# Gate/up pairs with five quads of seven products instead of four, in a two-layer encoder trunk

## The chip, the core and the metric

The kernel runs on one core of a Trainium2 chip. The metric is the device time of one execution in microseconds (us). The engines of the core that matter here are TensorE (PE, matrix products; PEld its weight loads), VectorE (DVE), ScalarE (ACT), GpSimd (POOL) and SyncE (SP), which issues most of the DMAs. Each has its own stream of instructions in program order, and they wait for each other through semaphores.

## The reference

The reference is a trunk of two layers on 256 tokens of width 2048, in float32. Each layer normalizes, projects, does differential attention in eight heads and a short gated convolution, projects back, and then does a SwiGLU block with an inner width of 5632. The change touches that block alone:

```python
h = rmsnorm(x, norm_ffn[l])
x = x + (jax.nn.silu(h @ w_gate[l]) * (h @ w_up[l])) @ w_down[l]
```

All products are float32. The kernel gets this accuracy from three products of a reduced kind (float32r): with each operand split into a high part (rounded) and a low part (the rest), it adds high x high, high x low and low x high.

## The kernel before

**Blocks, units and parts.** A weight matrix is cut into blocks of 512 columns, and a block into units of 256 rows (two tiles of 128). In the gate/up matrix a block holds 256 gate and 256 up columns, and two blocks, left and right, make a pair; there are 11 pairs in each layer and eight units in a block. For a unit SyncE loads a tile of 128 x 1024 into `raw`, ScalarE rounds it into `whi` (the high part, `split`, L761), VectorE subtracts and writes `wlo` (the low part, `split`, L1184), and TensorE does its products with both (L1861 to L1863): 3 for each of two tiles and two halves of the tokens, 12 for a unit and 24 for the same unit of left and right. There are four places in `raw` (each of four tiles, 1 MB) and five slots in `whi` and `wlo`, taken in turn.

**Quads.** Some units of left and right are taken together as a quad, which needs seven block products instead of eight (21 matmuls instead of 24, L1873 to L1875), as in Strassen's scheme. For this the sums of weight tiles must be made and split too. One quad has four steps on VectorE: `first_parts` (low parts of 1024 and of 512), `first_sum` (L1199, 512, into `raw`), `other_sums` (L1206, 1024, into `raw`) and `second_parts` (two low parts of 1024 of what the sums left there). The low parts of a quad stand at L1191 and the matching high parts, by ScalarE, at L767. The sum of two right tiles is made by a DMA that adds into `raw`, issued by GpSimd (`add_b`, L687) once the tile h has landed. The matching sums of the normed tokens are called forms. They are made once in a layer, in batches of two quads, by `form_sums` and `form_low` (VectorE) and `form_high` (ScalarE), in the last two blocks of the output projection, and lie where later pairs write their results.

**Order of a pair.** Of the 11 pairs the first nine after the first (1 to 9) are alike: four quads (units 0 to 3) and the units 4 to 7 of both sides; pair 0 differs in its head, pair 10 has two quads. The orders are written out by hand, once for each engine (`gu_four` and `gu_rest`), and must agree in the order in which slots are taken. VectorE begins a pair with the end of the one before it: `gu_fold` (L1281 to L1285), which puts the seven sums together as soon as ScalarE has copied the first of them out of PSUM (`sum_out`, L818), `gates_ups` (L1295) and `hidden_products` (L1558). GpSimd makes two low parts in a pair, unit 4 of left and of right (L693, `split_first_units`), once that same sum has been copied, and in between the adding DMAs. After `gu_rest` the next pair follows; then the down projection, which has its own quads.

Of the kernel before, what the change touches and what calls it, by code (L numbers as in the profile page):

```python
# [30 lines left out]
NCH = DM // COLS  # L31
# [24 lines left out]
GU_SEVENS = 4  # L56
DOWN_SEVENS = 10
FORM_BATCH = 2
GU_BATCHES = -(-GU_SEVENS // FORM_BATCH)
GU_FIRST_ORDER = [("left", 4), ("right", 4), ("left", 5), ("first", 0), ("first", 1), ("second", 0), ("first", 2),  # L60
# [5 lines left out]
GU_FOURS = range(1, NGU // 2 - 1)  # L66
POOL_UNIT = 4
# [109 lines left out]
class Pair:  # L177
    def __init__(self, plan, i, blocks, order, turns=None):
# [6 lines left out]
        self.first, self.fours = order is GU_FIRST_ORDER, order in (GU_FIRST_ORDER, GU_FOUR_ORDER)  # L185
        self.quad_loads = {}
        if self.fours:
            self.load_four(plan)
        for part, k in order:
            if part == "first":  # L190
                q = self.quads[k] = Quad(self, k)
                q.number = plan.quads
                plan.quads += 1
                q.loads = self.quad_loads[k] if self.fours else plan.next_place()
                plan.places[q.raw()] += 1
                q.added = plan.places[q.raw()]
# [3 lines left out]
            else:  # L200
                plan.unit(blocks[part == "right"], k, by_pool=self.fours and not self.first and k == POOL_UNIT)

        self.sums_taken = plan.taken[max(q.split[-1] for q in self.quads.values())][1]

    def load_four(self, plan):

        def place_of_units(k, place):
            for half, block in enumerate(self.blocks):
                block.load[k] = Load(plan, place, half)

        def place_of_quad(k, place):
            self.quad_loads[k] = [Load(plan, place, 0), Load(plan, place, 1)]
# [5 lines left out]
        place_of_units(4, a)  # L218
        place_of_quad(0, b)
        place_of_quad(1, c)  # L220
        place_of_units(5, d)
        place_of_quad(2, a)
        self.blocks[0].load[6] = Load(plan, d, 0, whole=False)
        place_of_quad(3, b)
        self.blocks[1].load[6] = Load(plan, d, 1, whole=False)
        place_of_units(7, c)
        plan.rotation = [a, d, b, c]


class Plan:  # L230
    def __init__(self):
# [15 lines left out]
        for layer in range(DEPTH):  # L247
            for name, n, by_tokens, units in (("qk", NQK, False, UNITS), ("v", NV, True, UNITS),
# [3 lines left out]
                for i in range(n):  # L252
# [7 lines left out]
                    elif i % 2:  # L260
                        if name == "gu":
                            pair = Pair(self, i // 2, made[-2:], GU_FOUR_ORDER if i // 2 in GU_FOURS
                                        else GU_LAST_ORDER if i == NGU - 1 else GU_FIRST_ORDER)
# [39 lines left out]
def build_program(nc, x, x_t_d, w_in, w_out, w_gu, w_down, consts_d, lambdas_d, tables_d, ident_d, gain_d, out):  # L303
# [49 lines left out]
    def share(name, shape, dtype):  # L353
# [44 lines left out]
               "gu": [(shared_end - 4 * FORM, shared_end - 2 * FORM, 2), (shared_end - 8 * FORM, shared_end - 6 * FORM, 2)]}  # L398
# [143 lines left out]
    with nc.Block() as block:  # L542

        @block.sync
        def _(sp):
# [69 lines left out]

            first, second = plan.blocks[:2]
# [14 lines left out]
            for blk in plan.blocks[2:]:  # L631
                if isinstance(blk, Pair) and blk.fours:
                    load_four(blk)
                elif isinstance(blk, Pair):
# [11 lines left out]
        def _(pool):  # L646
# [49 lines left out]
            def split_first_units(prior, pair):  # L696
                pool.wait_ge(sum_copied, prior.number + 1)
                for blk in pair.blocks:
                    split(blk, POOL_UNIT)

            pool.wait_ge(set_up, 2)
            for layer in range(DEPTH):
# [46 lines left out]
        def _(act):  # L749
# [159 lines left out]
            def gu_rest(pair):  # L909
# [12 lines left out]
                split(right, 7, 8)  # L922
                sum_out(pair)

            def gu_four(pair, prior):
# [4 lines left out]
                split(left, 4, 5)  # L930
                split(right, 4, 5)
# [11 lines left out]
                split(left, 5, 6)  # L943
                gu_rest(pair)
# [53 lines left out]
            for layer in range(DEPTH):  # L998
# [92 lines left out]
                for c in range(1, NCH):  # L1091
# [6 lines left out]
                    if c >= NCH - GU_BATCHES:  # L1098
                        split(blk, 6, 7)
                        form_high(layer, "gu", c - (NCH - GU_BATCHES))  # L1100
# [18 lines left out]
                for p in GU_FOURS:  # L1119
                    prior, pair = pair, plan.pairs[layer, "gu", p]  # L1120
                    gu_four(pair, prior)
# [57 lines left out]
        def _(dve):  # L1179
# [142 lines left out]
            def gu_rest(pair):  # L1322
# [18 lines left out]
                split(left, 7, 8)  # L1341
                split(right, 7, 8)
                gu_fold(pair)
                gates_ups(pair, 0, 0)

            def gu_four(pair, prior):
# [17 lines left out]
                split(left, 5, 6)  # L1364
                hidden_low(layer, before[1])
                gu_rest(pair)
# [232 lines left out]
            for layer in range(DEPTH):  # L1599
# [111 lines left out]
                for c in range(1, NCH):  # L1711
# [5 lines left out]
                    if c >= NCH - GU_BATCHES:  # L1717
                        split(blk, 4, 6)
                        form_sums(layer, "gu", c - (NCH - GU_BATCHES))
# [562 lines left out]
```

## Time and profile before

| what | value |
|---|---|
| device time, median of 3 runs | 2156.34 us |
| lowest, highest | 2155.99 us, 2157.56 us |
| span of the profiled execution | 2155.3 us |
| TensorE busy | 2144.2 us, 99% |
| VectorE busy | 1771.7 us, 82% |
| ScalarE busy | 1218.7 us, 57% |
| GpSimd busy | 314.5 us, 15% |
| a middle gate/up pair, fold to fold | 41.74 us |

The profile is of one execution, whose own time is the span, 1.0 us under the median of the timed runs. Busy time is the time covered by an engine's instructions. Two instructions that follow each other in an engine's pipeline overlap in their records, so the pace of an engine is read from the distance of their starts. The idle time in front of an instruction is given in brackets, with the instruction that released it.

### The profile page before, as it was taken

The numbers are of one execution on the slowest core, as the hardware profiler recorded it, in microseconds if no ns is written. First come the engines' busy times: TensorE is split into PE (matmuls) and PEld (weight loads), VectorE is DVE, ScalarE is ACT, GpSimd is POOL, SyncE is SP. The second block draws the span as 40 slices with busy tenths as digits, with TensorE's granted clock in tenths as the row PEclk, the third lists the DMA queues.
The fourth block names the chain that finished last, engine by engine and source line by source line (L and its number), as shares of the span: only waits on it lengthen the run. The fifth ranks groups of instructions, "written<-read, shape, count | busy, mean of one in ns | idle before, by whom it ended". The sixth has DMA issues, their size and how long they took to land.

```text
span 2155.3 us, 27924 instructions
## 1 busy us (share of the span) xinstructions
PE 2144.2 (99%) x10397; PEld 1794.4 (83%) x10397; DVE 1771.7 (82%) x2143; ACT 1218.7 (57%) x1714; POOL 314.5 (15%) x310
## 2 busy tenths in 40 slices
PE   9999999999999999999999999999999999999998
PEld 7888888888888888888888888888888888888886
DVE  5776676899899988999866666768998998988997
ACT  6454455666566555556554555546665665655564
POOL 0031120211221110000001211201112112100010
PEclk9999999999999999999999999999999999999999
DMA  9654445777777776767766444557777777756685
GB/s 349 203 183 176 176 157 189 212 218 223 246 217 229 227 229 205 227 216 221 246 200 217 171 161 157 176 194 212 218 229 232 219 222 244 221 198 219 219 240 181
DMA packets 152872, 456.81 MB, mean 212 GB/s; under 512 B 17440, under 2 KB 18080, under 8 KB 152352
## 3 DMA queue, kind: packets, MB, share of 16 engines
q1 hardware_dynamic: 132624, 416.41, 55.5%
q0 software_dynamic: 18816, 35.66, 9.8%
q10 hardware_dynamic: 1296, 2.94, 0.4%
q8 instruction: 83, 1.36, 0.2%
q14 instruction: 53, 0.43, 0.1%
HBM read 448.65 MB, written 2.10 MB: 209 GB/s over the span
## 4 chain that ended last, share of the span: by engine, by line
PE 97%; DVE 1%; ACT 1%; DMA 1%; POOL 0%; issue 0%; ACTq 0%; SPq 0%; DVEq 0%
PE bank L1861 16%; PE bank L1863 16%; PE bank L1862 16%; PE bank L1835 14%; PE bank L1875 9%; PE bank L1874 9%; PE bank L1873 9%; PE bank L1838 7%; PE bank L2039 1%; PE bank L1998 1%; PE bank L2021 1%; PE bank L1977 0%; DMA raw<-w_gu_dram 0%; POOL o_rms L675 0%; DVE wlo L1191 0%; PE bank L2007 0%
## 5 line engine op out<-in xcount | busy, mean ns | idle before, releaser
L761 ACT ACTIVATE whi<-raw 128x1024 fp32r<-128x1024 f32 x540 | 553.9, 1056 | 195.2 <-PE bank L1863 137.4
L1184 DVE TENSOR_TENSOR wlo<-raw,whi 128x1024 fp32r<-128x1024 f32 x504 | 606.9, 1229 | 65.9 <-ACT whi L761 64.9
L767 ACT ACTIVATE whi<-raw 128x1024 fp32r<-128x1024 f32 x480 | 430.0, 944 | 241.7 <-DVE raw L1206 139.6
L1191 DVE TENSOR_TENSOR wlo<-raw,whi 128x1024 fp32r<-128x1024 f32 x480 | 501.0, 1084 | 49.7 <-ACT whi L767 46.4
L1835 PE MATMUL bank<-xg,whi 128*128 128x512 f32 x1280 | 406.9, 399 | 1.0 <-DVE wlo L1440 1.0
L1861 PE MATMUL bank<-whi,xg 128*128 128x512 f32 x864 | 339.3, 393 | 0.5 <-DVE wlo L1184 0.5
L1863 PE MATMUL bank<-whi,xg 128*128 128x512 f32 x864 | 336.7, 390 | 0.0
L1862 PE MATMUL bank<-wlo,xg 128*128 128x512 f32 x864 | 336.5, 389 | 0.0
L1838 PEld LDWEIGHTS bank<-xg,wlo 128*128 128x128 f32 x1280 | 240.5, 188 | 56.9
L1838 PE MATMUL bank<-xg,wlo 128*128 128x256 f32 x1280 | 252.0, 278 | 0.0
L1835 PEld LDWEIGHTS bank<-xg,whi 128*128 128x128 f32 x1280 | 195.0, 189 | 3.3 <-DVE xg L1434 1.4
L1861 PEld LDWEIGHTS bank<-whi,xg 128*128 128x128 f32 x864 | 162.3, 188 | 34.8 <-DVE wlo L1184 1.6
L1863 PEld LDWEIGHTS bank<-whi,xg 128*128 128x128 f32 x864 | 162.2, 188 | 33.9
L1862 PEld LDWEIGHTS bank<-wlo,xg 128*128 128x128 f32 x864 | 162.3, 188 | 32.6
L687 POOL DMA_DIRECT2D raw<-w_gu_dram x84 | 72.6, 864 | 747.6 <-DMA raw<-w_gu_dram 747.6
L1861 PE MATMUL bank<-whi,hidden 128*128 128x512 f32 x416 | 162.5, 391 | 0.0
L1863 PE MATMUL bank<-whi,hidden 128*128 128x512 f32 x416 | 161.9, 389 | 0.0
L1862 PE MATMUL bank<-wlo,hidden 128*128 128x512 f32 x416 | 161.9, 389 | 0.0
L1206 DVE TENSOR_TENSOR raw<-raw 128x1024 f32<-128x1024 f32 x120 | 145.9, 1215 | 0.9
L1873 PE MATMUL bank<-whi,form_hi_gu 128*128 128x512 f32 x336 | 130.7, 389 | 0.0
L1875 PE MATMUL bank<-whi,form_lo_gu 128*128 128x512 f32 x336 | 130.7, 389 | 0.0
L1874 PE MATMUL bank<-wlo,form_hi_gu 128*128 128x512 f32 x336 | 130.7, 389 | 0.0
(161 smaller groups left out, 3050.7 us busy)
## 6 DMA issues: line engine op xcount, KB each, us to landing
raw<-w_gu_dram SPq DMA_DIRECT2D x268, 512.0 KB, 4.9
raw<-w_in_dram SPq DMA_DIRECT2D x188, 512.0 KB, 4.5
raw<-w_down_dram SPq DMA_DIRECT2D x140, 512.0 KB, 5.4
raw<-w_gu_dram SPq DMA_DIRECT2D x168, 256.0 KB, 4.2
raw<-w_out_dram SPq DMA_DIRECT2D x64, 512.0 KB, 4.4
raw<-w_gu_dram POOLq DMA_DIRECT2D x84, 256.0 KB, 5.7
raw<-w_down_dram SPq DMA_DIRECT2D x72, 256.0 KB, 4.7
raw<-w_down_dram POOLq DMA_DIRECT2D x36, 256.0 KB, 6.1
```

Of the source, the lines that this page charges most:

```text
L761: act.activation(whi[:, blk.slot(k)], raw[:, slot, half * UNIT_KT:(half + 1) * UNIT_KT, :], ACT.Copy).then_inc(hi_ready, 1)
L767: act.activation(whi[:, quad.slot(n), 0:tiles.stop - tiles.start], raw[:, quad.raw(), tiles, :], ACT.Copy).then_inc(hi_ready, 1)
L1184: dve.tensor_tensor(wlo[:, blk.slot(k)], raw[:, slot, half * UNIT_KT:(half + 1) * UNIT_KT, :], lo_bits(whi[:, blk.slot(k)]), ALU.subtract) ...
L1191: dve.tensor_tensor(wlo[:, quad.slot(n), into], raw[:, quad.raw(), tiles, :], lo_bits(whi[:, quad.slot(n), into]), ALU.subtract).then_inc( ...
L1835: pe.matmul(b[j][:], whi[:, blk.slot(k), i, w[j]], moving[:, kt, :], start=(kt == 0), stop=False, skip_group_check=True)
L1838: done = pe.matmul(b[j][:, 0:S], wlo[:, blk.slot(k), i, w[j]], moving[:, kt, 0:S], start=False, stop=final, skip_group_check=True)
L1861: pe.matmul(b[:], x_hi, w_hi, start=(n == UNIT_KT * blk.first_unit), stop=False)
L1862: pe.matmul(b[:], x_hi, w_lo, start=False, stop=False)
L1863: done = pe.matmul(b[:], x_lo, w_hi, start=False, stop=final)
L1873: pe.matmul(into[:], x_hi, w_hi, start=start, stop=False)
L1874: pe.matmul(into[:], x_hi, w_lo, start=False, stop=False)
L1875: return pe.matmul(into[:], x_lo, w_hi, start=False, stop=stop)
```

## The change

Pairs 1 to 8 of each layer take five quads instead of four (units 0 to 4) and units 5 to 7 instead of 4 to 7, in a new order on all engines (`GU_FIVE_ORDER`, `gu_five_rest`) and with a new order of the places in `raw` (`load_five`). Pair 9 keeps four quads. A third batch of forms, for the fifth quad alone, is made at the end of pair 0. GpSimd makes unit 5 of both sides as it made unit 4, and also the low part of right 7 of a pair with five quads: `split_last_unit` waits until VectorE has made that of left 7.

```diff
-GU_SEVENS = 4
+GU_SEVENS = 5
...
+GU_FIVE_ORDER = [("left", 5), ("right", 5), ("first", 0), ("first", 1), ("left", 6), ("second", 0), ("first", 2),
+                 ("second", 1), ("first", 3), ("right", 6), ("second", 2), ("first", 4), ("second", 3), ("second", 4),
+                 ("left", 7), ("right", 7)]
+GU_MIDDLE = range(1, NGU // 2 - 1)
+GU_FIVES = range(1, NGU // 2 - 2)
...
+    def load_five(self, plan):
+
+        a, b, c, d = plan.rotation
+        self.place_of_units(plan, 5, a)
+        self.place_of_quad(plan, 0, b)
+        self.place_of_quad(plan, 1, c)
+        self.place_of_quad(plan, 2, d)
+        self.place_of_units(plan, 6, a)
+        self.place_of_quad(plan, 3, b)
+        self.place_of_quad(plan, 4, c)
+        self.place_of_units(plan, 7, d)
...
+            def split_last_unit(pair):
+                left, right = pair.blocks
+                wait_for_split(pool, left.split[UNITS - 1])
+                split(right, UNITS - 1)
...
-                for p in GU_FOURS:
+                for p in GU_MIDDLE:
                     prior, pair = (plan.pairs[layer, "gu", n] for n in (p - 1, p))
                     add_b(pair.quads[0])
+                    if prior.fives:
+                        split_last_unit(prior)
                     split_first_units(prior, pair)
...
                 second_parts(q3)
                 split(left, 7, 8)
+                if pair.first:
+                    form_sums(pair.layer, "gu", GU_BATCHES - 1)
                 split(right, 7, 8)
+                if pair.first:
+                    form_low(pair.layer, "gu", GU_BATCHES - 1)
                 gu_fold(pair)
...
+            def gu_five_rest(pair):
+
+                left, right = pair.blocks
+                q0, q1, q2, q3, q4 = (pair.quads[k] for k in range(5))
+                first_sum(q1)
+                second_parts(q0)
+                first_parts(q2)
+                other_sums(q1)
+                second_parts(q1)
+                first_sum(q2)
+                first_parts(q3)
+                other_sums(q2)
+                split(right, 6, 7)
+                second_parts(q2)
+                first_sum(q3)
+                first_parts(q4)
+                other_sums(q3)
+                second_parts(q3)
+                first_sum(q4)
+                other_sums(q4)
+                second_parts(q4)
+                split(left, 7, 8)
+                gu_fold(pair)
+                gates_ups(pair, 0, 0)
```

VectorE in the middle of such a pair before the change, around the sums of q1 (L1206 is other_sums, L1184 the low part of a unit, L1191 those of a quad, L1199 first_sum):

```order
L1191 TENSOR_TENSOR wlo<-raw,whi 128x512 [waits hi_ready]
L1206 TENSOR_TENSOR raw<-raw 128x2x512 [waits first_sums,weights_ready]
L1184 TENSOR_TENSOR wlo<-raw,whi 128x1024 [waits hi_ready]
L1191 TENSOR_TENSOR wlo<-raw,whi 128x1024 [waits hi_ready] x2
L1199 TENSOR_TENSOR raw<-raw 128x512 [waits b_added0,weights_ready]
```

The same place of a pair with five quads in the changed program (L1272 is other_sums, L1257 a quad's low parts, L1265 first_sum):

```order
L1257 TENSOR_TENSOR wlo<-raw,whi 128x512 [waits hi_ready]
L1272 TENSOR_TENSOR raw<-raw 128x2x512 [waits first_sums,weights_ready]
L1257 TENSOR_TENSOR wlo<-raw,whi 128x1024 [waits hi_ready] x2
L1265 TENSOR_TENSOR raw<-raw 128x512 [waits b_added3,weights_ready]
L1257 TENSOR_TENSOR wlo<-raw,whi 128x1024 [waits hi_ready]
```

The low part of right 5 is gone from between the sums of q1 and its second parts; what follows them is as before.

VectorE at the end of a pair before the change, from q2's second parts to the fold (L1281):

```order
L1191 TENSOR_TENSOR wlo<-raw,whi 128x1024 [waits hi_ready] x2
L1199 TENSOR_TENSOR raw<-raw 128x512 [waits b_added3,weights_ready]
L1184 TENSOR_TENSOR wlo<-raw,whi 128x1024 [waits hi_ready]
L1206 TENSOR_TENSOR raw<-raw 128x2x512 [waits first_sums,weights_ready]
L1191 TENSOR_TENSOR wlo<-raw,whi 128x1024 [waits hi_ready] x2
L1184 TENSOR_TENSOR wlo<-raw,whi 128x1024 [waits hi_ready] x2
L1281 TENSOR_TENSOR gate_up<-gate_up,bank 128x512 [waits sum_copied]
```

The same stretch with five quads, from the last of q4's first parts to the fold (L1250 is the low part of a unit, L1347 the fold):

```order
L1257 TENSOR_TENSOR wlo<-raw,whi 128x512 [waits hi_ready]
L1272 TENSOR_TENSOR raw<-raw 128x2x512 [waits first_sums,weights_ready]
L1257 TENSOR_TENSOR wlo<-raw,whi 128x1024 [waits hi_ready] x2
L1265 TENSOR_TENSOR raw<-raw 128x512 [waits b_added2,weights_ready]
L1272 TENSOR_TENSOR raw<-raw 128x2x512 [waits first_sums,weights_ready]
L1257 TENSOR_TENSOR wlo<-raw,whi 128x1024 [waits hi_ready] x2
L1250 TENSOR_TENSOR wlo<-raw,whi 128x1024 [waits hi_ready]
L1347 TENSOR_TENSOR gate_up<-gate_up,bank 128x512 [waits sum_copied]
```

A second set of sums, that of q4, with its second parts has come in behind q3's, and one low part of a unit instead of two stands in front of the fold.

GpSimd in a middle pair before, with the two low parts at its head (L693) and the adding DMAs (L687):

```order
L693 TENSOR_TENSOR wlo<-raw,whi 128x1024 [waits hi_ready,sum_copied]
L693 TENSOR_TENSOR wlo<-raw,whi 128x1024 [waits hi_ready]
L687 DMA raw<-w_gu_dram 128x512 [waits h_landed3]
L687 DMA raw<-w_gu_dram 128x512 [waits h_landed0]
L687 DMA raw<-w_gu_dram 128x512 [waits h_landed2]
L687 DMA raw<-w_gu_dram 128x512 [waits h_landed1]
```

GpSimd in the changed program, from the last adding DMA of a pair with five quads (L724) through the DMA of the next pair's q0 and the three low parts (L730):

```order
L724 DMA raw<-w_gu_dram 128x512 [waits h_landed1]
L730 TENSOR_TENSOR wlo<-raw,whi 128x1024 [waits hi_ready,weights_ready]
L730 TENSOR_TENSOR wlo<-raw,whi 128x1024 [waits hi_ready,sum_copied]
L730 TENSOR_TENSOR wlo<-raw,whi 128x1024 [waits hi_ready]
L724 DMA raw<-w_gu_dram 128x512 [waits h_landed2]
L724 DMA raw<-w_gu_dram 128x512 [waits h_landed3]
L724 DMA raw<-w_gu_dram 128x512 [waits h_landed1]
```

The low part of right 7 stands behind the DMA of the next pair's first quad and ahead of the two that were there; it waits for VectorE (weights_ready), and only the next one for the copied sum.

## Rows read from the trace of the kernel before

**Rows 1.** The page: busy time by engine, and the chain of waits by engine.

```profile
PE 2144.2 (99%) x10397; PEld 1794.4 (83%) x10397; DVE 1771.7 (82%) x2143; ACT 1218.7 (57%) x1714; POOL 314.5 (15%) x310
...
PE 97%; DVE 1%; ACT 1%; DMA 1%; POOL 0%; issue 0%; ACTq 0%; SPq 0%; DVEq 0%
```

**Rows 2.** Windows of two middle pairs, fold to fold: busy us by engine.

```profile
589.88:631.62 41.74, 41.74 (x190) 34.58 (x189) 38.23 (x43) 25.36 (x32) 8.17 (x6) 1.00 0.74 227
631.62:673.37 41.75, 41.75 (x190) 34.59 (x189) 38.24 (x44) 25.36 (x32) 8.20 (x6) 1.00 0.74 228
```

**Rows 3.** Timeline of TensorE: start and length in us, line, operation.

```profile
628.07 0.39 PE L1873 MATMUL bank<-whi,form_hi_gu 128*128 128x512 f32 x1
...
630.57 0.39 PE L1875 MATMUL bank<-whi,form_lo_gu 128*128 128x512 f32 x1
```

**Rows 4.** Timeline of VectorE, the end of a middle pair, idle in brackets.

```profile
620.94 0.68 DVE L1199 TENSOR_TENSOR raw<-raw 128x512 f32<-128x512 f32 x1
621.54 1.22 DVE L1184 TENSOR_TENSOR wlo<-raw,whi 128x1024 fp32r<-128x1024 f32 x1
622.68 1.22 DVE L1206 TENSOR_TENSOR raw<-raw 128x1024 f32<-128x1024 f32 x1
625.07 2.36 DVE L1191 TENSOR_TENSOR wlo<-raw,whi 128x1024 fp32r<-128x1024 f32 x2 [1.17 <-ACT whi L767]
627.35 2.35 DVE L1184 TENSOR_TENSOR wlo<-raw,whi 128x1024 fp32r<-128x1024 f32 x2
631.62 0.69 DVE L1281 TENSOR_TENSOR gate_up<-gate_up,bank 128x512 f32<-128x512 f32 x1 [1.92 <-ACT gate_up L818]
```

**Rows 5.** Timeline of VectorE, the same pair from its fold on.

```profile
589.88 0.69 DVE L1281 TENSOR_TENSOR gate_up<-gate_up,bank 128x512 f32<-128x512 f32 x1 [1.90 <-ACT gate_up L818]
...
605.26 4.08 DVE L1191 TENSOR_TENSOR wlo<-raw,whi 128x1024 fp32r<-128x1024 f32 x4
609.26 1.21 DVE L1206 TENSOR_TENSOR raw<-raw 128x1024 f32<-128x1024 f32 x1
...
616.27 1.22 DVE L1206 TENSOR_TENSOR raw<-raw 128x1024 f32<-128x1024 f32 x1
...
618.66 2.36 DVE L1191 TENSOR_TENSOR wlo<-raw,whi 128x1024 fp32r<-128x1024 f32 x2
```

**Rows 6.** Timeline of ScalarE in the same pair.

```profile
610.55 3.48 ACT L767 ACTIVATE whi<-raw 128x1024 fp32r<-128x1024 f32 x4 [1.56 <-PE bank L1875]
...
623.98 2.01 ACT L767 ACTIVATE whi<-raw 128x1024 fp32r<-128x1024 f32 x2 [3.42 <-DVE raw L1206]
```

**Rows 7.** Timeline of GpSimd, its two low parts of that pair.

```profile
590.94 4.77 POOL L693 TENSOR_TENSOR wlo<-raw,whi 128x1024 fp32r<-128x1024 f32 x2 [4.11 <-ACT whi L761]
```

**Rows 8.** Hidden products by line in that pair: ns min, median, max.

```profile
L1558 DVE SCALAR_TENSOR_TENSOR ev<-gate_up,rms_tok,ev x4: 468/471/701, 595.3 to 597.8; 128x256 f32<-128x256 f32 x4
```

**Rows 9.** A quad's h load by its line, L583, in the pairs.

```profile
DMA to landing us min/median/max: 2.6/3.0/5.2
```

**Rows 10.** A quad's left load by its line, L585, in the pairs.

```profile
DMA to landing us min/median/max: 3.7/5.4/6.7
```

**Rows 11.** Timeline of VectorE in the first gate/up pair.

```profile
391.75 0.68 DVE L1199 TENSOR_TENSOR raw<-raw 128x512 f32<-128x512 f32 x1
392.54 1.23 DVE L1206 TENSOR_TENSOR raw<-raw 128x1024 f32<-128x1024 f32 x1
...
422.89 0.69 DVE L1281 TENSOR_TENSOR gate_up<-gate_up,bank 128x512 f32<-128x512 f32 x1 [1.75 <-ACT gate_up L818]
```

**Rows 12.** Groups by form, two steps of the gate/up forms: busy, mean.

```profile
L1274 DVE TENSOR_TENSOR form_lo_gu<-form_sum_gu,form_hi_gu 128x1024 fp32r<-128x1024 f32 x4 | 4.9, 1226 | 0.0
...
L1258 DVE TENSOR_TENSOR ev<-xg 128x1024 f32<-128x1024 f32 x4 | 4.9, 1219 | 0.0
```

**Rows 13.** Windows of the last stretches: PEclk is the granted clock.

```profile
2145.00:2150.00 5.00, 2.12 (x10) 1.43 (x8) 2.99 (x7) 1.76 (x3) 1.88 (x2) 1.00 0.26 105
2150.00:2155.00 5.00, 0.00 (x0) 0.00 (x0) 0.75 (x1) 1.15 (x1) 0.00 (x1) 0.67 0.79 315
```

More of the change, by code:

```diff
@@ L200, in __init__, with place_of_units, place_of_quad @@
             else:
-                plan.unit(blocks[part == "right"], k, by_pool=self.fours and not self.first and k == POOL_UNIT)
+                plan.unit(blocks[part == "right"], k, by_pool=(part, k) in self.pool_units)
         self.sums_taken = plan.taken[max(q.split[-1] for q in self.quads.values())][1]
-    def load_four(self, plan):
[L207 to L212, printed above, removed]
+    def place_of_units(self, plan, k, place):
+        for half, block in enumerate(self.blocks):
+            block.load[k] = Load(plan, place, half)
+    def place_of_quad(self, plan, k, place):
+        self.quad_loads[k] = [Load(plan, place, 0), Load(plan, place, 1)]
+    def load_four(self, plan):
         if self.first:
@@ L614, in load_four, with load_five @@
                 load(right, 7)
+            def load_five(pair):
+                left, right = pair.blocks
+                load(left, 5)
+                load(right, 5)
+                for k in range(3):
+                    load_quad(pair.quads[k])
+                load(left, 6)
+                load(right, 6)
+                load_quad(pair.quads[3])
+                load_quad(pair.quads[4])
+                load(left, 7)
+                load(right, 7)
             first, second = plan.blocks[:2]
@@ L929, in gu_four @@
                 before = [b.i for b in prior.blocks]
-                split(left, 4, 5)
-                split(right, 4, 5)
+                k = 5 if pair.fives else 4
+                split(left, k, k + 1)
+                split(right, k, k + 1)
                 silu(prior.layer, before[0], 0)
@@ L2056, in gu_rest, with gu_five_rest, gu_middle @@
                 plain(right, 7)
-            def gu_four(pair):
+            def gu_five_rest(pair):
                 left, right = pair.blocks
-                plain(left, 4)
+                q0, q1, q2, q3, q4 = (pair.quads[k] for k in range(5))
+                second_products(q0)
+                first_products(q2)
+                second_products(q1)
+                first_products(q3)
+                plain(right, 6)
+                second_products(q2)
+                first_products(q4)
+                second_products(q3)
+                second_products(q4)
+                plain(left, 7)
+                plain(right, 7)
+            def gu_middle(pair):
+                left, right = pair.blocks
+                k = 5 if pair.fives else 4
+                plain(left, k)
                 turn_hidden(pair.layer, 2 * pair.i - 2)
-                plain(right, 4)
+                plain(right, k)
                 turn_hidden(pair.layer, 2 * pair.i - 1)
```

105 lines of the change are left out of this document (70 added, 35 removed).

## The prediction

> **What bounds the kernel now.** I read the page first: TensorE is busy 99% of the span and the chain of waits is 97% TensorE [rows 1]. Then the windows of two middle gate/up pairs, from one fold on VectorE to the next: 41.74 and 41.75 us, with TensorE busy in all of it and VectorE in 38.23 and 38.24 [rows 2]. The reader is to see two things there. A pair lasts as long as its matmuls; and VectorE, which makes nearly all low parts, has only some 3.5 us to spare.
>
> That TensorE sets the pair is better seen in the timeline than in its busy share, because its records overlap: the first and the last of twelve matmuls start 2.50 us apart, so they follow each other every 0.227 us though each is recorded with 0.39 [rows 3]. A middle pair has four quads of 21 products and four unit pairs of 24, 180 in all: 40.9 us, and the eight transposes of the hidden blocks fill the rest of 41.74.
>
> Next the timeline of VectorE at the end of such a pair [rows 4]. A low part of 1024 starts 1.14 us after the one before (621.54 to 622.68), two take 2.28 (625.07 to 627.35), a 512 one 0.60 (620.94 to 621.54). VectorE stands still in two places that matter: 1.92 before the fold, which waits for ScalarE's copy of a sum that TensorE finishes late, and 1.17 at 625.07, which is the row to remember. There other_sums(q3) (L1206) is followed directly by second_parts(q3) (L1191). The second parts are split from what other_sums has just written, and ScalarE must round them first: it starts at 623.98, 0.08 after other_sums ends [rows 6], and VectorE goes on 1.09 later. From other_sums to the next low part are 2.39 us (622.68 to 625.07) in which VectorE works 1.22. For q0, q1 and q2 another low part stands in between and covers this: for q2 the same 2.39 (616.27 to 618.66) hold other_sums and a whole unit [rows 5].
>
> **The change, part by part.**
>
> TensorE. In each of the 16 pairs (8 in each layer) one unit pair of 24 products becomes a quad of 21: 3 x 0.227 = 0.68 us off, a pair of 41.06, 10.9 us in all. This is a gain only where TensorE stays the bound.
>
> VectorE, work. The pair loses three 1024 low parts (right 5 of old, left or right 6, and right 7, that goes to GpSimd; units left to it fall from six to three): 3 x 1.14 = 3.42. It gains a quad: three 1024 low parts, one of 512, first_sum of 512 and other_sums of 1024: 4 x 1.14 + 2 x 0.60 = 5.76. Net 2.34 us more, on 38.23: 40.6 of the 41.06 that TensorE would need. Taken alone that would just fit.
>
> VectorE, stalls. The new order has only one unit left between the sums, right 6, and it covers q2. Behind other_sums of q1, q3 and q4 the second parts follow directly, so the 1.17 comes three times instead of once: 2.34 us more. This is in the order of the code, and ScalarE cannot start sooner than the sums are written. Together 4.7 us more in a pair with 3.5 us of idle time, and the 1.17 in these cannot be used up. So VectorE, with ScalarE's copies in its loop, is the new bound, and I follow it from fold to fold on the clock of the pair in [rows 4, 5].
>
> Fold at 589.88; up to 605.26 the order is as before with left 6 in the place of left 5: 15.38 us. Second parts of q0 and first parts of q2 up to 609.26, 4.00, also as before. From there:
> - q1: other_sums and stall 2.39, second parts 2.28: 613.93.
> - first_sum(q2) 0.60 and first parts of q3, 4.00 - 2.28 = 1.72: 616.25.
> - other_sums(q2) and right 6, 2.39; second parts of q2, 2.28: 620.92.
> - first_sum(q3) and first parts of q4, 2.32: 623.24.
> - q3: 2.39 + 2.28: 627.91.
> - first_sum(q4), at once followed by other_sums(q4), which reads it: 0.79 as in the first pair (391.75 to 392.54) [rows 11]: 628.70. other_sums and stall 2.39, second parts 2.36 to the end of the second: 633.45.
> - TensorE gets the first of these two at 632.31, starts 0.08 later and works twelve products; the twelfth starts 11 x 0.227 after, at 634.89. In the trace the fold starts 1.05 after such a twelfth (630.57 to 631.62) [rows 3, 4]. VectorE's low part of left 7 lies beside this.
> The fold comes at 635.94 instead of 631.62: 4.32 us later in each pair, 16 x 4.32 = 69.1 us. TensorE is then idle some 5 us in each pair, mainly before q3 and q4 and in front of right 6.
>
> The third batch of forms stands in the first pair of each layer between VectorE's last two low parts, where the fold then waits 1.75 us [rows 11]. For two quads the batch has steps of 1.22 and 1.23 [rows 12], one of 512 elements at 0.69 and two smaller ones, at most 4.5 together; for one quad it is between half and all of that, 2.2 to 4.5. I take 2.7, near the half, since the part of a step that doesn't shrink is small in the rows (1.22 against 0.68 for half the elements). Less the 1.75, it puts that fold off by 0.95; twice, 1.9 us (bounds 0.9 to 5.5).
>
> GpSimd. It makes two low parts in 4.77 [rows 7] and gets a third, right 7. It may start when left 7 is through, 634.5, and not when the sum is copied, so its three end near 634.6 + 7.16 = 641.8, 5.8 us behind the fold, as the two do now (595.71, behind 589.88). TensorE wants right 7 twelve products after left 7, at 637.8, and gets it at 637.0. Cost 0, with 0.8 us of cover. Ahead of it in GpSimd's queue now stands the accumulating DMA of the next pair's q0, which waits for the h load; this is issued when q3 is through, near 628, and lands in 2.6 to 5.2 us [rows 9]: 630.6 to 633.2, before 634.5. If that cover goes, TensorE waits for right 7, and VectorE's gate/up additions behind it (third rival).
>
> What GpSimd does to VectorE: of the four hidden products of a pair one takes 701 ns, where the median is 471, and the first starts at 595.3, while GpSimd still works [rows 7, 8]. The Trainium skill, page "SBUF — State Buffer", section "Who interferes with whom", says that a VectorE instruction with two SBUF inputs and a GpSimd one that reads SBUF exclude each other. The trace agrees with this (230 ns). By it the third low part speaks against the change as far as it ends later behind the fold than the two do now, which is 0.03 us here and 0.5 us over all pairs; without such a rule it is 0.
>
> Loads. q3 goes into the place of q0 and its left tile must land before ScalarE copies it. The place is free when the second parts of q0 are through, 605.26 + 2.36 = 607.6, as before; ScalarE must start by 613.4, 1.09 before VectorE wants q3 (613.93 + 0.60). Landing takes 3.7, 5.4, 6.7 us (least, median, most) [rows 10], issued 0.4 behind the place: up to 1.3 late. In the pair shown ScalarE copies q3 near 612.5, the third of four without a pause from 610.55 [rows 6], and no more traffic is added there, so 0; the upper bound is 16 x 1.3 = 21 us.
>
> **The sum.** 69.1 + 1.9 = 71.0 on the profiled 2155.3: 2226.3. The median of the three timed runs, 2156.34, lies 1.0 above the span of the profile, so 2227.4.
>
> **The rivals.**
> TensorE stays the bound. For it: it is the bound in all of the trace, and what VectorE works, 40.6, is under 41.06. It would give 2156.3 - 10.9 = 2145.4. Against it: 1.17 three times and 38.23 + 2.34 do not fit into 41.06. This is the other side; it decides from the point where VectorE's stalls shrink below 0.2 us each.
> The two new stalls don't come, because ScalarE's copy turns out covered: 16 x 2.34 less, 2190. Against it: the row at 625.07 is the same code and no cover stands there.
> GpSimd is late with right 7, by up to one low part of 2.39, in each pair: 16 x 2.39 more, 2266. For it: a third low part and a DMA in front; against it the 0.8 us.
> TensorE's clock falls. It is granted 1.00 throughout the pairs [rows 2], since it never pauses there. In the last stretches it is 1.00 with 2.12 us of work in 5, and 0.67 only where it does nothing [rows 13]. At 1.2 instead of 2.4 GHz the twelve products ahead of the fold would come every 0.454: an estimate of 2.7 us a pair from rows 3, 44 in all, 2271. The Trainium skill, page "TensorE: Matmul & The Clock Gate", section "A second HAM failure mode: psum-queue depth-cycling", tells that short pauses between groups of matmuls can make the clock swing; no trace here shows it yet.
>
> **How the numbers follow.** Forecast 0.76, with a range of its own from 2214 (tail 0.8 us shorter in each pair) to 2249 (late loads); TensorE stays the bound 0.05; stalls covered 0.06; GpSimd late 0.08; clock 0.05. Forecast and covered stalls together give 0.82 from 2190 to 2250. About 0.2% is what a measurement of this kernel can tell from no change. Faster is the first rival, 0.05; within it what lies between that and the others, 0.02; slower 0.93.
>
> **What would show it.** In the changed profile: middle pairs of 46 us; VectorE idle 1.2 us three times in each before a second part, released by ScalarE; idle gaps of TensorE released by VectorE's low parts; granted clock 1.00. Wrong would be: pairs near 41 us; right 7 released by GpSimd as the longest wait; the pairs with four quads, the down or the in projection longer than before.

## The result and the profile after

The changed kernel takes 2252.74 us (median of 4 runs, 2251.92 to 2253.87) against 2156.16 for the kernel before (4 runs): ratio 1.0445, 95% interval 1.0433 to 1.0458, 96.6 us slower. The forecast was 2227.4, with a range of its own from 2214 to 2249. The direction is as forecast, and 25.3 us are missing from the sum.

The page of the kernel after, busy time by engine and the chain of waits by engine, which answers to [rows 1]:

```profile
PE 2179.4 (97%) x10349; PEld 1796.9 (80%) x10349; DVE 1816.3 (81%) x2201; ACT 1242.4 (55%) x1748; POOL 367.3 (16%) x342
...
PE 79%; DVE 12%; issue 5%; ACT 4%; POOL 0%; DMA 0%; ACTq 0%; DVEq 0%
```

TensorE's share of the chain falls from 97% to 79%, and VectorE, ScalarE and "issue" take what it lost. TensorE has 48 matmuls less and is still busy 35 us longer, which needs an explanation: some of its matmuls may have become slower.

Windows of the kernel after: a middle pair with five quads, and pair 9, which keeps four. Columns as in [rows 2]: the window, its length, busy us of PE, PEld, DVE, ACT and POOL, then the granted clock, DMA share and GB/s.

```profile
661.75:709.53 47.78, 44.02 (x187) 34.77 (x186) 40.77 (x46) 26.72 (x34) 11.45 (x8) 0.96 0.69 203
...
805.11:846.86 41.75, 41.75 (x190) 34.58 (x189) 38.25 (x43) 25.39 (x32) 8.18 (x6) 1.00 0.72 223
```

A pair with five quads lasts 47.78 instead of 41.74: 6.04 more, and 16 x 6.04 = 96.6, which is the whole change. Pair 9 is as it was. The reader should also see the clock: 0.96 over the new pair, 1.00 in pair 9.

VectorE in the first of these two pairs, from fold to fold (L1272 is other_sums, L1257 a quad's low parts, L1250 a unit's low part, L1347 the fold), as [rows 4, 5] of before:

```profile
661.75 0.69 DVE L1347 TENSOR_TENSOR gate_up<-gate_up,bank 128x512 f32<-128x512 f32 x1 [3.00 <-ACT gate_up L862]
...
681.15 1.22 DVE L1272 TENSOR_TENSOR raw<-raw 128x1024 f32<-128x1024 f32 x1
683.55 2.36 DVE L1257 TENSOR_TENSOR wlo<-raw,whi 128x1024 fp32r<-128x1024 f32 x2 [1.18 <-ACT whi L811]
...
695.17 1.22 DVE L1272 TENSOR_TENSOR raw<-raw 128x1024 f32<-128x1024 f32 x1
697.57 2.36 DVE L1257 TENSOR_TENSOR wlo<-raw,whi 128x1024 fp32r<-128x1024 f32 x2 [1.18 <-ACT whi L811]
...
700.64 1.23 DVE L1272 TENSOR_TENSOR raw<-raw 128x1024 f32<-128x1024 f32 x1
703.04 2.36 DVE L1257 TENSOR_TENSOR wlo<-raw,whi 128x1024 fp32r<-128x1024 f32 x2 [1.17 <-ACT whi L811]
705.31 1.22 DVE L1250 TENSOR_TENSOR wlo<-raw,whi 128x1024 fp32r<-128x1024 f32 x1
709.53 0.69 DVE L1347 TENSOR_TENSOR gate_up<-gate_up,bank 128x512 f32<-128x512 f32 x1 [3.00 <-ACT gate_up L862]
```

The stall, 1.17 to 1.18, stands three times, behind other_sums of q1, q3 and q4. The second parts of q4 end at 705.40, 43.65 after the fold; the prediction's chain had 43.57. Up to here it held. What follows did not: the next fold comes 4.13 after that end, where 2.49 were forecast, and the wait in front of it is 3.00.

TensorE at that place (L1972 to L1974 are a quad's matmuls):

```profile
701.48 0.39 PE L1974 MATMUL bank<-whi,form_lo_gu 128*128 128x512 f32 x1
704.32 0.79 PE L1972 MATMUL bank<-whi,form_hi_gu 128*128 128x512 f32 x1 [2.44 <-DVE wlo L1257]
704.91 0.63 PE L1973 MATMUL bank<-wlo,form_hi_gu 128*128 128x512 f32 x1
...
707.04 0.63 PE L1972 MATMUL bank<-whi,xg 128*128 128x512 f32 x1
707.47 0.47 PE L1973 MATMUL bank<-wlo,xg 128*128 128x512 f32 x1
...
708.47 0.39 PE L1974 MATMUL bank<-whi,form_lo_gu 128*128 128x512 f32 x1
```

TensorE stands still for 2.44 us until the first of q4's second parts is there, and then its matmuls follow each other every 0.43 us (the first after 0.59) until 707.47 and about every 0.23 after 707.78. From the first to the last of the twelve are 4.15, where 2.50 were assumed [rows 3]. The last starts at 708.47 and the fold 1.06 later, as assumed.

The windows around it (columns as above; after the five engines stands the granted clock):

```profile
701.00:703.00 2.00, 0.87 (x4) 0.38 (x2) 0.86 (x1) 1.05 (x2) 0.00 (x0) 1.00 0.72 189
703.00:705.00 2.00, 0.68 (x2) 0.59 (x3) 1.96 (x2) 2.00 (x4) 0.86 (x1) 0.81 1.01 322
705.00:707.00 2.00, 2.00 (x6) 1.55 (x5) 1.53 (x2) 0.85 (x1) 0.38 (x1) 0.50 0.93 165
707.00:709.00 2.00, 2.00 (x9) 1.60 (x8) 0.00 (x0) 0.10 (x1) 2.00 (x1) 0.84 0.91 293
709.00:711.00 2.00, 2.00 (x11) 1.65 (x10) 1.40 (x3) 2.00 (x3) 0.41 (x1) 1.00 0.87 287
```

The granted clock is 1.00 up to 703, the first part of the pause with it, and 0.50 (1.2 GHz) in the stretch behind the pause, where only six matmuls have a part in the 2 us, against eleven in the last of these windows. So it looks as if an idle time that VectorE causes is paid for a second time behind it; the first four experiments test that.

### The profile page after: what moved, and what is told of

Read it like the earlier page. It is cut to its first block, busy times and chain, and to the rows that moved or that the text cites. A ratio compares the mean times of both kernels' runs of the same rounds, so it can differ in the third digit from the quotient of the medians.

```text
span 2251.1 us, 28048 instructions
## 1 busy us (share of the span) xinstructions
PE 2179.4 (97%) x10349; PEld 1796.9 (80%) x10349; DVE 1816.3 (81%) x2201; ACT 1242.4 (55%) x1748; POOL 367.3 (16%) x342
## 4 chain that ended last, share of the span: by engine, by line
PE 79%; DVE 12%; issue 5%; ACT 4%; POOL 0%; DMA 0%; ACTq 0%; DVEq 0%
PE bank L1934 13%; PE bank L1960 12%; PE bank L1962 12%; PE bank L1961 12%; PE bank L1972 7%; DVE wlo L1257 7%; PE bank L1937 7%; PE bank L1974 6%; PE bank L1973 6%; ACT whi L811 4%; DVE raw L1272 2%; DVE raw L1265 1%; PE bank L2138 1%; PE bank L2097 1%; PE bank L2120 1%
## 5 line engine op out<-in xcount | busy, mean ns | idle before, releaser
L811 ACT ACTIVATE whi<-raw 128x1024 fp32r<-128x1024 f32 (+1 forms) x544 | 485.5, 944 | 352.7 <-DVE raw L1272 158.7
L1257 DVE TENSOR_TENSOR wlo<-raw,whi 128x1024 fp32r<-128x1024 f32 (+1 forms) x544 | 568.6, 1088 | 83.2 <-ACT whi L811 80.6
L805 ACT ACTIVATE whi<-raw 128x1024 fp32r<-128x1024 f32 x508 | 520.2, 1056 | 155.6 <-PE bank L1962 98.0
L1250 DVE TENSOR_TENSOR wlo<-raw,whi 128x1024 fp32r<-128x1024 f32 x456 | 551.0, 1233 | 65.5 <-ACT whi L805 64.5
L1960 PE MATMUL bank<-whi,xg 128*128 128x512 f32 x736 | 291.4, 396 | 7.6 <-DVE wlo L1250 7.6
L1962 PE MATMUL bank<-whi,xg 128*128 128x512 f32 x736 | 287.0, 390 | 0.0
L1961 PE MATMUL bank<-wlo,xg 128*128 128x512 f32 x736 | 286.9, 390 | 0.0
L1972 PE MATMUL bank<-whi,form_hi_gu 128*128 128x512 f32 x400 | 169.8, 425 | 53.2 <-DVE wlo L1257 53.2
L724 POOL DMA_DIRECT2D raw<-w_gu_dram x100 | 87.3, 917 | 784.8 <-DMA raw<-w_gu_dram 784.8
L1960 PEld LDWEIGHTS bank<-whi,xg 128*128 128x128 f32 x736 | 138.2, 188 | 42.9 <-DVE wlo L1250 14.9
L1272 DVE TENSOR_TENSOR raw<-raw 128x1024 f32<-128x1024 f32 x136 | 166.1, 1222 | 2.6
L1973 PE MATMUL bank<-wlo,form_hi_gu 128*128 128x512 f32 x400 | 163.7, 409 | 0.0
L1974 PE MATMUL bank<-whi,form_lo_gu 128*128 128x512 f32 x400 | 163.5, 409 | 0.0
L1962 PEld LDWEIGHTS bank<-whi,xg 128*128 128x128 f32 x736 | 138.2, 188 | 29.4
```

Of the source, the lines that this page charges most:

```text
L805: act.activation(whi[:, blk.slot(k)], raw[:, slot, half * UNIT_KT:(half + 1) * UNIT_KT, :], ACT.Copy).then_inc(hi_ready, 1)
L811: act.activation(whi[:, quad.slot(n), 0:tiles.stop - tiles.start], raw[:, quad.raw(), tiles, :], ACT.Copy).then_inc(hi_ready, 1)
L1250: dve.tensor_tensor(wlo[:, blk.slot(k)], raw[:, slot, half * UNIT_KT:(half + 1) * UNIT_KT, :], lo_bits(whi[:, blk.slot(k)]), ALU.subtract) ...
L1257: dve.tensor_tensor(wlo[:, quad.slot(n), into], raw[:, quad.raw(), tiles, :], lo_bits(whi[:, quad.slot(n), into]), ALU.subtract).then_inc( ...
L1960: pe.matmul(b[:], x_hi, w_hi, start=(n == UNIT_KT * blk.first_unit), stop=False)
L1961: pe.matmul(b[:], x_hi, w_lo, start=False, stop=False)
```

## The experiments

Two theories stood against each other at first. One: the new pair is VectorE's loop, three uncovered round trips to ScalarE in it, and the idle time that they give TensorE lowers its clock. The other: GpSimd's third low part, or the loads of the new order of places, hold the pair up. Times of the kernel before beside the experiments are 2156.18 to 2156.49.

**All three round trips covered.** VectorE's order alone is changed, so that a low part of another quad stands between other_sums and the second parts of q1, q3 and q4. All work is as in the changed kernel.

```diff
-                first_parts(q2)
                 other_sums(q1)
+                first_parts(q2)
                 second_parts(q1)
...
-                second_parts(q2)
+                split_quad(q2, 2, slice(2, 4))
                 first_sum(q3)
-                first_parts(q4)
+                split_quad(q2, 3, slice(0, 2))
                 other_sums(q3)
-                second_parts(q3)
+                first_parts(q4)
+                split_quad(q3, 2, slice(2, 4))
                 first_sum(q4)
                 other_sums(q4)
+                split_quad(q3, 3, slice(0, 2))
                 second_parts(q4)
```

> The changed kernel with other_sums of q1, q3 and q4 moved ahead on VectorE so that at least one other low part stands between the sums of each quad and its second parts; nothing is added or taken away. Theory (VectorE's chain with ScalarE's round trip, and a lowered TensorE clock behind the longest gap): the three stalls of 1.17 go, the gap in front of q4's second parts shrinks and the clock stays at 1.00; by the steps of the chain a pair takes 42.4 us instead of 47.8, so 2156.2 + 16 x 0.7 = 2167 us. Rival 'work' (VectorE's 2.3 us of added work alone make it the bound): little changes, 2240 to 2253. Rival 'GpSimd' (its third low part, or the port it shares with VectorE, holds the pair): no change, 2253.

Measured: 2179.62 (2176.39 to 2181.63), ratio 1.0107 (1.0092 to 1.0122), mean clock 0.999. An order of instructions on one engine gives back 73 of the 96.6 us, though the time stays 12.6 above the 2167 that was expected. The pairs are no longer alike: the shortest takes 42.76, the longest 44.62. TensorE's longest wait in the longest pair (what it waited for: us in total, times, longest):

```profile
PE bank L1962 <- POOL wlo L730: 1.1, 1, 1.1
...
```

Here TensorE does wait for GpSimd's right 7, the prediction's third rival. It is the only one of the sixteen pairs in which TensorE stands still for GpSimd, so it does not explain the others: in the pair of 43.75, ScalarE waits 1.27 for the load of left 6, and VectorE 0.75 behind it.

**The round trip of q4 alone.**

```diff
                 other_sums(q3)
-                second_parts(q3)
+                split_quad(q3, 2, slice(2, 4))
                 first_sum(q4)
                 other_sums(q4)
+                split_quad(q3, 3, slice(0, 2))
                 second_parts(q4)
```

> The same for q4 alone: other_sums(q4) is moved in between the two second parts of q3. Theory: one stall of 1.17 goes, and with it the 2.5 us gap of TensorE that is followed by the lowered clock, so a pair loses 1.2 + 1.7 and takes 44.9 us: 2207 us, granted clock 1.00. If the lowered clock were not tied to this gap: 1.2 less for each pair, 2234 us with a clock below 1.00. Rival 'GpSimd': 2253.

Measured: 2217.40 (2215.43 to 2219.03), ratio 1.0283 (1.0268 to 1.0298), pairs of 45.22 to 45.79, about 0.5 longer than the 44.9 expected. A middle pair of it, by windows:

```profile
650.22:695.60 45.38, 42.58 (x187) 33.62 (x186) 40.92 (x47) 26.69 (x34) 11.57 (x9) 1.00 0.71 214
```

Its TensorE at the second low part of q3, which VectorE now makes behind other_sums(q4) (L1973 to L1975 are a quad's matmuls here):

```profile
688.73 0.39 PE L1975 MATMUL bank<-whi,form_lo_gu 128*128 128x512 f32 x1
690.51 0.50 PE L1973 MATMUL bank<-whi,xg 128*128 128x512 f32 x1 [1.39 <-DVE wlo L1257]
690.86 0.40 PE L1974 MATMUL bank<-wlo,xg 128*128 128x512 f32 x1
691.10 0.40 PE L1975 MATMUL bank<-whi,xg 128*128 128x512 f32 x1
```

The longest pause has moved from q4 to q3 and is 1.39 instead of 2.44; q4's matmuls follow q3's without a pause, from 692.02 on. The first matmul behind the pause takes 0.35 to the next and the others 0.23 to 0.24, and the pair's clock is 1.00. One stall of 1.17 cost 47.78 - 45.38 = 2.4 us, twice its length, since the fall of the clock went with it.

**The clock alone.** Ten bf16 products of zeros are added into a sum while TensorE waits for q4's second parts. They add nothing, and VectorE's order stays that of the changed kernel with all three stalls.

```diff
+    zeros = put("zeros", [P, 16], BF16)
...
                 second_products(q3)
+                for _ in range(10):
+                    pe.matmul(SUM_AH[:], zeros[:, 0:1].to_broadcast([P, P]), zeros[:, 0:1].to_broadcast([P, COLS]), start=False, stop=False)
                 second_products(q4)
```

> The changed kernel with ten products of zeros added by TensorE in front of q4's second products, where it waits 2.45 us for VectorE; they add nothing to the sum that they go to. Theory: the ten fit into the gap, TensorE's granted clock stays at 1.00, the twelve products behind come every 0.23 us and not 0.43, and a pair takes 46.1 instead of 47.8: 2225 us. If the clock has no part in it, or does not depend on this gap: 2253.

Measured: 2229.79 (2229.26 to 2230.59), ratio 1.0341 (1.0325 to 1.0356), mean clock 0.999, pairs of 46.21 to 46.27 (the first of a layer 46.51 and 46.46). TensorE of it, at the same place (L2171 are the zeros):

```profile
694.83 2.36 PE L2171 MATMUL bank<-zeros 128*128 128x512 bf16 x10
697.43 0.50 PE L1974 MATMUL bank<-whi,form_hi_gu 128*128 128x512 f32 x1 [0.25 <-DVE wlo L1258]
697.77 0.39 PE L1975 MATMUL bank<-wlo,form_hi_gu 128*128 128x512 f32 x1
...
700.06 0.39 PE L1976 MATMUL bank<-whi,form_lo_gu 128*128 128x512 f32 x1
```

VectorE's folds at both ends of a pair of it (L1348), 46.23 apart:

```profile
654.89 0.69 DVE L1348 TENSOR_TENSOR gate_up<-gate_up,bank 128x512 f32<-128x512 f32 x1 [1.51 <-ACT gate_up L863]
...
701.12 0.69 DVE L1348 TENSOR_TENSOR gate_up<-gate_up,bank 128x512 f32<-128x512 f32 x1 [1.47 <-ACT gate_up L863]
```

The window of the twelve matmuls behind the zeros:

```profile
697.43:700.29 2.86, 2.86 (x13) 2.36 (x14) 2.22 (x2) 1.54 (x2) 0.56 (x1) 1.00 0.81 129
```

The twelve matmuls now take 2.63 from first to last at a clock of 1.00, and a middle pair is 1.54 shorter (47.78 to 46.24) although ten matmuls were added. This isolates the clock: 16 x 1.54 = 24.6 us by the middle pairs. The device time fell by 22.95, since the mean gain of all sixteen pairs is 1.50 and the first pair begins 0.5 later here. That is nearly all of what was missing from the sum. The pair that is left, 46.24, is close to the forecast one (41.74 + 4.32 = 46.06).

**GpSimd's third low part taken back.** Right 7 goes to VectorE again, behind left 7.

```diff
-        if self.fives:
-            self.pool_units = self.pool_units + order[-1:]
...
-                    if prior.fives:
-                        split_last_unit(prior)
...
                 split(left, 7, 8)
+                split(right, 7, 8)
```

> The changed kernel with the low part of right 7 made by VectorE again; GpSimd makes two in a pair as in the kernel before. Theory: it falls into the 3 us in which VectorE waits for the fold, 2253 us within 3. Rival 'GpSimd' (third low part late, or VectorE held by the shared port): faster, up to 16 x 2.4 = 38 us, 2215. Rival 'work' (VectorE has no idle time that counts): slower by 16 x 1.14 = 18, 2271.

Measured: 2252.91 (2250.86 to 2254.64), ratio 1.0446 (1.0428 to 1.0463): no difference. The fold of VectorE in this kernel:

```profile
710.99 0.69 DVE L1343 TENSOR_TENSOR gate_up<-gate_up,bank 128x512 f32<-128x512 f32 x1 [1.94 <-ACT gate_up L858]
```

The wait before the fold shrinks from 3.00 to 1.94: VectorE does the low part in idle time. GpSimd is not the cause, and giving it the unit bought nothing.

This kernel also shows the clock by itself. Its first two new pairs of the second layer, by windows:

```profile
1544.87:1591.34 46.47, 41.88 (x182) 32.62 (x181) 41.76 (x49) 27.27 (x35) 9.05 (x7) 1.00 0.70 204
1591.34:1639.16 47.82, 44.06 (x187) 34.75 (x186) 41.89 (x47) 26.68 (x34) 9.08 (x7) 0.96 0.72 214
```

In both TensorE stands still before q4's second parts, for 2.43 and for 2.45 us. Behind the first pause the clock stayed at 1.00 and the matmuls came 0.23 apart. Behind the second they came 0.43 apart from the fourth on. Of the 32 such pauses of this kernel and the changed one (2.41 to 2.45 us), 31 were followed by slow matmuls and this one was not. What decides it no run here shows.

**Two stalls put into the kernel before.** Nothing but VectorE's order is changed there, so that q1 and q2 lose the unit that stood in their round trip.

```diff
-                other_sums(q1)
                 split(right, 5, 6)
+                other_sums(q1)
                 second_parts(q1)
                 first_sum(q2)
                 first_parts(q3)
-                other_sums(q2)
                 split(left, 6, 7)
+                other_sums(q2)
                 second_parts(q2)
```

> The kernel before the change (four quads) with other_sums of q1 and q2 moved behind the low part that covered them, so that VectorE stands 1.17 us twice more in each of the 20 pairs that use this order; no work is added. Theory: VectorE finishes q3 2.34 us later, at 629.77 on the clock of the pair shown; the fold then comes 2.5 after, at 632.3 instead of 631.6: a pair takes 42.4 instead of 41.74, 20 x 0.64 = 13 us, 2169, at a clock of 1.00. Most of the 2.34 is lost in the idle time in front of the fold. Rival 'work' (only added work counts, stalls are absorbed): 2156.

Measured: 2170.62 (2170.61 to 2172.44), ratio 1.0069 (1.0052 to 1.0086), mean clock 0.999, most pairs 42.42 to 42.48. VectorE of it:

```profile
658.96 2.36 DVE L1191 TENSOR_TENSOR wlo<-raw,whi 128x1024 fp32r<-128x1024 f32 x2 [1.18 <-ACT whi L767]
...
667.11 2.36 DVE L1191 TENSOR_TENSOR wlo<-raw,whi 128x1024 fp32r<-128x1024 f32 x2 [1.18 <-ACT whi L767]
...
678.47 0.69 DVE L1281 TENSOR_TENSOR gate_up<-gate_up,bank 128x512 f32<-128x512 f32 x1 [0.33 <-ACT gate_up L818]
```

Two stalls of 1.18 are 2.36 us of VectorE's time. The wait before the fold gave back 1.92 - 0.33 = 1.59 of it, and the pair became 0.7 longer; twenty pairs have this order, which is the 14 us. A stall costs 0.35 here, where there is slack, and 2.4 where there is none and the clock falls.

**Stalls covered and right 7 back.** The first and the fourth edit together, which leaves only the added work.

```diff
# VectorE's order as in the first experiment, then
                 split(left, 7, 8)
+                split(right, 7, 8)
```

> The kernel with the three stalls covered (first experiment) and right 7 made by VectorE again. In the first experiment pairs took 42.9 to 44.6 us; in the longer ones TensorE waited up to 1.1 for GpSimd's right 7, which stands behind a DMA that waits for a load. Theory: without it all pairs take 42.9, since VectorE's right 7 falls into the 1.6 us in front of the fold: 2156.2 + 16 x 1.15 = 2175 us. Rival (the added low part counts on VectorE): 16 x 1.14 more than the first experiment, 2198.

Measured: 2172.44 (2171.89 to 2173.65), ratio 1.0075 (1.0060 to 1.0090), pairs of 42.66 to 42.90. VectorE's waits over nearly seven pairs (470 to 760 us):

```profile
DVE gate_up L1343 <- ACT gate_up L858: 2.8, 6, 0.5
DVE gate_up L1357 <- PE bank L1961: 1.6, 7, 0.2
```

VectorE now works without a pause but for 0.7 us a pair. Right 7 itself costs nothing here: the wait before the fold was 1.57 in the first experiment and is 0.44 to 0.47 now, and most pairs are a little shorter than the shortest there (42.76). The times differ by 7.2 us, so right 7 on GpSimd cost that much once the stalls were covered; how, apart from the one wait of 1.1, is not shown. What still separates this pair from 41.74, 0.96 us, would then be VectorE's work ahead of q4's second parts; the next two take work away to see.

**Less work at the end of the loop.** As above, with the two second low parts of q4 made for 16 of the 512 columns.

```diff
-                second_parts(q4)
+                split_quad(q4, 2, slice(2, 4), slice(0, 16))
+                split_quad(q4, 3, slice(0, 2), slice(0, 16))
```

> The kernel of the row above (stalls covered, right 7 on VectorE) in which VectorE makes only 16 of 512 columns of the two low parts of q4's second parts; the rest of these low parts keeps old values, so this part of the gate/up sums is not computed. It takes some 2.1 us of work from VectorE in each pair and leaves all waits and orders. Theory: VectorE's chain falls to 40.8, below what TensorE needs, and TensorE is the bound again at 41.06 a pair: 2156.2 - 10.9 = 2145 us, the saving of the 48 products at last. Rival (loads, or ScalarE, set the pair): 2165 or more, no better than a few us under the row above.

Measured: 2172.08 (2171.49 to 2172.54), ratio 1.0073 (1.0058 to 1.0088), pairs of 42.66 to 42.71 (the first of a layer 42.94 and 42.89): a miss, nothing was gained. VectorE at the end of a pair:

```profile
630.72 1.45 DVE L1253 TENSOR_TENSOR wlo<-raw,whi 128x1024 fp32r<-128x1024 f32 x2
632.92 0.19 DVE L1253 TENSOR_TENSOR wlo<-raw,whi 128x32 fp32r<-128x32 f32 x1 [0.76 <-ACT whi L807]
633.88 2.36 DVE L1246 TENSOR_TENSOR wlo<-raw,whi 128x1024 fp32r<-128x1024 f32 x2 [0.76 <-ACT whi L801]
637.08 0.69 DVE L1343 TENSOR_TENSOR gate_up<-gate_up,bank 128x512 f32<-128x512 f32 x1 [0.85 <-ACT gate_up L858]
```

Its ScalarE there (L807 rounds the quads' tiles, L801 the units'):

```profile
630.89 2.00 ACT L807 ACTIVATE whi<-raw 128x1024 fp32r<-128x1024 f32 x2 [2.80 <-DVE raw L1268]
632.80 1.99 ACT L801 ACTIVATE whi<-raw 128x1024 fp32r<-128x1024 f32 x2
```

The work that was cut is itself the cover of ScalarE's copies: it makes four in a row behind other_sums(q4), from 630.89 to 634.79, and VectorE waits 0.76 twice for them. The cut was made where work hides a round trip, so it tells nothing of work at other places.

**Less work at the head of the loop.** The kernel with covered stalls and right 7 on VectorE again; but now the first 1024 of q1 and the low part of left 6 are made for 16 columns; no copy by ScalarE is late there.

```diff
-                first_parts(q1)
+                few = slice(0, 16 if pair.fives else COLS)
+                split_quad(q1, 0, slice(0, 2), few)
+                split_quad(q1, 1, slice(2, 3))
                 other_sums(q0)
                 k = 6 if pair.fives else 5
-                split(left, k, k + 1)
+                split(left, k, k + 1, few)
```

> The kernel with covered stalls and right 7 on VectorE, in which VectorE makes only 16 of 512 columns of the first low part of q1 and of that of left 6, early in each pair with five quads; the rest of these low parts keeps old values, so this part of the gate/up sums is not computed. It takes the same 2.1 us from VectorE as the narrow low parts of q4 did, but at a place where ScalarE's copies are ahead and don't hang on sums. Theory (VectorE's work is what is left, and the narrow q4 only uncovered ScalarE's four copies in a row behind the last sums): the chain falls from 42.7 to 40.5, TensorE is the bound at 41.06 a pair, 2145 us, at most 2155 if the load of q1 comes late. Rival (a loop of ScalarE, PSUM and loads sets 42.7 whatever VectorE does): 2172 again.

Measured: 2152.71 (2151.97 to 2154.74), ratio 0.9983 (0.9974 to 0.9993), pairs of 41.46 to 41.80 (the first of a layer 40.84). The window over nearly seven pairs:

```profile
470.00:760.00 290.00, 288.95 (x1294) 237.02 (x1293) 278.39 (x329) 190.90 (x232) 62.88 (x50) 1.00 0.78 233
```

Its TensorE at the second low part of q3, the one behind other_sums(q4):

```profile
625.42 0.39 PE L1975 MATMUL bank<-whi,form_lo_gu 128*128 128x512 f32 x1
625.91 0.50 PE L1973 MATMUL bank<-whi,xg 128*128 128x512 f32 x1
626.25 0.40 PE L1974 MATMUL bank<-wlo,xg 128*128 128x512 f32 x1
```

Here TensorE is busy 99.6%, so with less work at the head of VectorE's loop the new pairs are TensorE's. They are 0.4 above the 41.06 of the prediction. In each pair one weight load waits for a low part, 4.0 us over seven pairs: the matmul at 625.91 starts 0.49 after the one before it and the next 0.34 after that, 0.38 more than two steps of 0.227. That is the size of the gap.

## Why the prediction missed its range

**What held.** The new bound, VectorE's loop with ScalarE in it: 43.65 to the end of q4's second parts (43.57 forecast), the three stalls of 1.17 to 1.18, and 46.24 for the pair at full clock (46.06). The gain of TensorE is real but not reached: it shows in the last experiment, where the pairs come down to 41.47 once VectorE has less to do. GpSimd's third low part cost nothing in this kernel, as the fourth experiment shows; with the stalls covered it cost 7.2 us. VectorE's hidden products beside its work also stayed as they were: of the four in a pair one takes 701 ns and the median 473 (before: 701 and 471). No load showed as a cost in the changed kernel: the eight new pairs of a layer are within 47.70 to 47.88.

**The step that failed.** The prediction put the clock at 1.00 for every matmul of its sum. A falling clock ("It is granted 1.00 throughout the pairs [rows 2], since it never pauses there") was a rival with a chance of 0.05. The reason given holds for the kernel before only; in a new pair the clock was 0.96. The prediction's own sum made TensorE idle some 5 us in each pair, and yet it took the clock of a TensorE that never pauses for the twelve matmuls behind the longest of these pauses. The clock was no rival of the forecast but a part of it. With the measured 1.54 a pair instead of 0 the sum becomes 2227.4 + 24.6 = 2252.0. The rival's own price, 2.7 a pair, was for all twelve matmuls at 1.2 GHz and gave 2271; about seven ran at that pace (0.43), and 7/12 x 2.7 = 1.6. The third experiment shows this by itself: keeping TensorE busy through the pause takes 1.54 off a middle pair with VectorE's order unchanged. The Trainium skill, page "TensorE: Matmul & The Clock Gate", section "A second HAM failure mode: psum-queue depth-cycling", tells of a kernel whose short idle times between groups of matmuls cost throughput through the clock; this trace agrees for the longest idle time of a pair, with 0.50 behind the 2.44 us, and not for the pauses of 0.34 to 0.50, behind which the matmuls kept their pace of 0.23.

**Smaller terms.** The third batch of forms was to put the first pair's fold off by 0.95 in each layer. It came at 422.91 instead of 422.89, and VectorE does not wait there:

```profile
419.47 0.68 DVE L1324 TENSOR_TENSOR ev<-xg 128x512 f32<-128x512 f32 x1
...
421.18 1.22 DVE L1250 TENSOR_TENSOR wlo<-raw,whi 128x1024 fp32r<-128x1024 f32 x1
422.31 0.68 DVE L1340 TENSOR_TENSOR form_lo_gu<-form_sum_gu,form_hi_gu 128x512 fp32r<-128x512 f32 x1
422.91 0.68 DVE L1347 TENSOR_TENSOR gate_up<-gate_up,bank 128x512 f32<-128x512 f32 x1
```

From start to start the batch takes 1.71 and 0.60, 2.31 in all (2.7 was taken). The old wait of 1.75 swallowed most of it, and VectorE came to its last second parts 0.45 sooner than before. So the 1.9 us of the sum are not there. The pair at full clock is 0.18 longer than forecast, 2.9 us in all, and it is luck that these two largely cancel.

**The 6.04 us of a pair, by the runs.** Each figure is the difference of the pairs of two kernels:

| part | from | us a pair | all 16 pairs |
|---|---|---|---|
| TensorE's clock behind the pause | 47.78 to 46.24, zeros added | 1.54 | 25 |
| q4's round trip, the clock apart | 46.24 to 45.38, q4 covered | 0.86 | 14 |
| q1's and q3's, with right 7 back on VectorE | 45.38 to 42.70, all covered | 2.68 | 43 |
| VectorE's added work ahead of q4's second parts | 42.70 to 41.74, what is left | 0.96 | 15 |

The last is what remains of the added work (2.34 us, and 1.14 for right 7, which fills the wait before the fold) after the idle time of the old pair was used up, and the saving of TensorE lies behind it. That this remainder is work is shown by the last experiment alone. How the price is shared between neighbouring rows depends on the order in which the edits are undone, since a stall costs more beside other stalls; only the sum does not.

No kernel that does the whole computation with five quads came below the kernel before; the nearest, 2172.44, is 0.75% above it. VectorE is busy 283.76 of 290 us in it, 41.8 a pair, which is above the 41.06 that TensorE would need. With right 7 on GpSimd it has less work, but the shortest pair of the first experiment is 42.76. Whether another order would pass below 41.74 was not tried.

## What to carry to other kernels

Before trading work of the busiest engine for work of the next one, lay out the next one's loop in program order with its round trips to other engines, and see which independent instruction covers each: here the instructions that the change took away were those covers. If the sum leaves TensorE idle, price the matmuls behind the longest pause at both levels of its clock, as a part of the forecast and not as a rival. And do not cut work to measure its cost where that work hides a wait.

## What was not expected of the hardware

One pause of 2.44 us in a pair of 47.78 was followed by a granted clock of 0.50, with the matmuls 0.43 apart for some 3 us; pauses of 0.34, 0.48 and 0.50 in the same pair, and of 1.39 with the q4 cover, were not, at 1.00. With right 7 taken back the fall came only two or three matmuls behind the pause, and once, behind 2.43 us, not at all. Ten bf16 products of zeros from a tile of 16 columns, 2.36 us in all, kept the clock at 1.00, and the float32 products behind them came every 0.23 from the second on.
